# Attention output through weights of products in two output halves, and one setup step for the last mixers

## The reference

```python
s = jnp.einsum("bthd,bshd->bhts", qb, k) * scale      # fox, a block of 128 queries
s = s + fb[..., :, None] - big_f[..., None, :]
s = jnp.where(k_pos[None, :] <= q_pos[:, None], s, -jnp.inf)
p = jax.nn.softmax(s, axis=-1)
return jnp.einsum("bhts,bshd->bthd", p, v)
...
sa = jnp.einsum("bhvk,bhk->bhv", state, -kk_t)        # rwkv, the mixer that runs beside it
state = (state * w_t[:, :, None, :] + sa[..., None] * (kk_t * a_t)[:, :, None, :]
         + v_t[..., None] * k_t[:, :, None, :])
```

```python
c = _rms_norm(a_ckv, kv_norm_g[layer])
lb_all = jnp.cumsum(jax.nn.softmax(lb_logits, axis=0), axis=0)
o_a = _dsa_mixer(a_q, c, a_iq, a_ik, a_iw, w_uk[layer], rel_bias)   # index scores, top 256, softmax
o_b = _hgrn2_mixer(b_q, b_f, b_i, lb_all[layer])
```

## Time and profile before

| | |
|---|---|
| time, median of 3 runs | 5380.27 us (5369.63 to 5392.05) |
| profiled execution | 5369.74 us, span 5368.1 us |
| mean granted clock of TensorE | 0.829 of 2.4 GHz |
| TensorE products busy | 4420.3 us (82% of the span) |
| VectorE, ScalarE, GpSimd busy | 2632.6, 1913.5, 738.0 us |
| fox and rwkv steps | from 1372.9 us to 2514.4 us of the span |
| setup of the second layer's mixers | from 3517.4 us to 3575.7 us of the span |

### The profile page before, as it was taken

How to read it: one execution, slowest core, us unless ns; L and a number is a source line. 1 busy time by engine, 2 the same in 40 slices (tenths; PEclk the granted TensorE clock), 3 DMA queues, 4 the chain that set the end, 5 groups by cost and what they waited for, 6 DMA issues and landing times. The chain is left out here.

```text
span 5368.1 us, 64565 instructions
## 1 busy us (share of the span) xinstructions
PE 4420.3 (82%) x23178; PEld 3238.0 (60%) x23178; DVE 2632.6 (49%) x5352; ACT 1913.5 (36%) x3894; POOL 738.0 (14%) x753
## 2 busy tenths in 40 slices
PE   7988999973678888987998999956688887876668
PEld 6876777762566666665446888833344454544557
DVE  3114444445555544542111111148998888887435
ACT  3112233234223223332111010123676767777511
POOL 3101111100000000000000000012222333444310
PEclk9998999975667677776999999976587887877779
DMA  5336666643010000001221212120000001011032
GB/s 180 124 123 231 210 209 216 215 155 123 24 34 23 23 23 12 23 14 69 85 84 69 81 65 81 54 61 23 17 19 18 18 18 36 18 36 36 30 129 103
DMA packets 199360, 417.95 MB, mean 78 GB/s; under 512 B 37032, under 2 KB 67404, under 8 KB 198876
## 3 DMA queue, kind: packets, MB, share of 16 engines
q1 hardware_dynamic: 199040, 413.81, 22.5%
HBM read 292.08 MB, written 121.65 MB: 77 GB/s over the span
## 5 line engine op out<-in xcount | busy, mean ns | idle before, releaser
L3131 POOL TENSOR_TENSOR ds_E<-ds_bT 128x256 f32<-128x256 f32 x112 | 71.8, 641 | 2928.5 <-ACT ds_bT L3100 2743.2
L2620 PE MATMUL ds_big<-ds_ikT,ds_iqT 64*128 64x512 f32 (+3 forms) x640 | 384.0, 747 | 94.9 <-ACT ds_iqT L2597 60.2
L272 PE MATMUL g_acc<-g_ws_hi,second_hT_hi 128*128 128x512 f32 (+1 forms) x1024 | 384.5, 375 | 11.8 <-DVE g_ws_lo L307 11.8
L273 PE MATMUL g_acc<-g_ws_lo,second_hT_hi 128*128 128x512 f32 (+1 forms) x1024 | 384.2, 375 | 0.0
L274 PE MATMUL g_acc<-g_ws_hi,second_hT_lo 128*128 128x512 f32 (+1 forms) x1024 | 384.1, 375 | 0.0
L475 PE MATMUL mm_big<-mm_gw_hi,mm_ghT_hi 128*128 128x512 f32 (+1 forms) x768 | 318.5, 415 | 31.2 <-PEq L134 31.2
L2683 DVE TENSOR_SCALAR_CACHE_REDUCE ds_eq<-ds_hi,ds_num 128x2048 uint16<-128x2048 uint16 (+13 forms) x224 | 331.3, 1479 | 26.2 <-issue 4.0
L286 DVE COPY g_stage<-g_acc 128x512 f32<-128x512 f32 (+1 forms) x64 | 41.6, 650 | 529.0 <-PE g_acc L274 529.0
L477 PE MATMUL mm_big<-mm_gw_hi,mm_ghT_lo 128*128 128x512 f32 (+1 forms) x768 | 299.7, 390 | 0.0
L476 PE MATMUL mm_big<-mm_gw_lo,mm_ghT_hi 128*128 128x512 f32 (+1 forms) x768 | 299.3, 390 | 0.0
L2723 ACT ACTIVATE ds_signs<-ds_lo,ds_at 128x2048 bf16<-128x2048 uint16 (+13 forms) x224 | 291.4, 1301 | 1.5 <-issue 0.4
(11 more groups left out here) (505 smaller groups left out, 10007.3 us busy)
## 6 DMA issues: line engine op xcount, KB each, us to landing
mm_ghT_hi<-turned SPq DMA_DIRECT2D x96, 512.0 KB, 4.0
mm_ghT_lo<-turned SPq DMA_DIRECT2D x96, 512.0 KB, 5.3
proj<-g_stage SPq DMA_DIRECT2D x112, 256.0 KB, 2.0
proj<-mm_gstage SPq DMA_DIRECT2D x80, 256.0 KB, 5.0
mm_x<-proj SPq DMA_DIRECT2D x64, 256.0 KB, 3.8
g_w<-in_w_in SPq DMA_DIRECT2D x56, 256.0 KB, 4.0
proj<-fp_stage SPq DMA_DIRECT2D x48, 256.0 KB, 2.0
mm_graw<-in_w_in SPq DMA_DIRECT2D x40, 256.0 KB, 6.5
```

Source lines behind the costliest of these rows:

```text
L272: pe.matmul(sums, hT.hi[:, k, tile], wt.hi[:, k, 0:width], start=(k == 0), stop=False)
L273: pe.matmul(sums, hT.hi[:, k, tile], wt.lo[:, k, 0:width], start=False, stop=False)
L2620: pe.matmul(big[:, n % 2, 0:wd], iqT[o, h // 2], b.ikT[o, x:x + wd], start=True, stop=True)\
```

## The change

Two edits are joined.

**Values as weights.** In steps with five key tiles or more (k from 4 to 15) the roles in `weigh` are exchanged. The values of a tile (128 keys by 64 dimensions) become the stationary operand, and the transposed softmax weights (128 columns) move. The result of an even tile goes to partitions 0 to 63 of bank 7 and that of an odd tile to partitions 64 to 127, so the two sums of a head lie in two output halves (`sums`), with dimensions on the partitions. At the end of the step ScalarE copies the bank to SBUF (`f_sums_kept`), and four products with `fold` (two identity matrices on top of each other) add the halves and turn them back to token order in bank 5 or 6. VectorE waits for these (`f_folded`) before it divides. `fold` is made by one VectorE instruction ahead of the steps.

**One setup step.** `last_mixers_setup` does in one step what `load`, the norm step, `hgrn_setup`, `threshold_setup` and the step of loads did. All 15 loads are issued at its start, and each engine waits for those that it needs. The temporary buffers of the old norm step are now places in buffers that the tiles use later. Half of the index-key transposes move ahead of the bias products and the other half behind them, and the copy of the transposed index keys moves from VectorE to ScalarE, in two parts.

```diff
@@ fox_attend
-    o = big[:, 7, 0:GW].rearrange("p (h d) -> p h d", h=HEADS)
+    sums = big[:, 7].rearrange("p (h t) -> p h t", h=HEADS)
+
+    folded = k >= FOLDED
...
+    if folded:
+        uses.append((("o",), None))
     turns = in_turn([5, 6], uses)
+    o = big[:, turns["o",][0] if folded else 7, 0:GW].rearrange("p (h d) -> p h d", h=HEADS)
...
         yield from keep(act, HEADS - 1)
+        if folded:
+            yield 11 / N
+            act.wait_ge(s.f_weighed, HEADS * NP)
+            act.activation(pT[:, 0], sums, ACT.Copy).then_inc(s.f_sums_kept, 1)
...
         yield 11 / N
         dve.wait_ge(s.f_exps, HEADS)
         dve.reciprocal(den[:], den[:])
-        dve.wait_ge(s.f_weighed, HEADS * NP)
+        if folded:
+            dve.wait_ge(s.f_folded, 1)
+        else:
+            dve.wait_ge(s.f_weighed, HEADS * NP)
...
+        if folded:
+            yield 11 / N
+            take(pe, "o")
+            pe.wait_ge(s.f_sums_kept, 1)
+            for h in range(HEADS):
+                m = pe.matmul(o[:, h], pT[:, 0, h], b.fold[:], start=True, stop=True)
+            m.then_inc(s.f_folded, 1)
...
         for t in range(wd // P):
-            m = pe.matmul(o[:, h], pT[:, (h * NP + p) % 2, t], b.v[:, x // P + t, h * HD:(h + 1) * HD],
-                          start=(p == 0 and t == 0), stop=(x + (t + 1) * P == W))
+            at = x // P + t
+            v, w = b.v[:, at, h * HD:(h + 1) * HD], pT[:, (h * NP + p) % 2, t]
+            if folded:
+                m = pe.matmul(sums[(LOW, HIGH)[at % 2], h], v, w, start=(at < 2), stop=(at + 2 > k))
+            else:
+                m = pe.matmul(o[:, h], w, v, start=(at == 0), stop=(at == k))
         m.then_inc(s.f_weighed, 1)
```

The new setup step, cut to its loads and the order of its work:

```diff
+        @block.sync
+        def _(sp):
+            for r in range(2):
+                sp.dma_start(ik[:, :, r], proj[:, E_IK:E_IK + IDX_DIM].rearrange("(t p) c -> p t c", p=P))\
+                  .then_inc(s.ik_in, 16)
+            sp.dma_start(ct[:], proj[:, E_C:E_C + R].rearrange("(t p) c -> p t c", p=P)).then_inc(s.c_in, 16)
+            sp.dma_start(g, row(w['kv_norm_g_2'])).then_inc(s.g_in, 16)
+            sp.dma_start(rb, w['rel_bias_2'], allow_slow_non_contiguous=True).then_inc(s.oh_in, 16)
+            sp.dma_start(oh, onehot).then_inc(s.oh_in, 16)
...
+            n = index_loads(ib, sp, s.rest_in, proj, TILES - 1) + attend_loads(ab, sp, s.rest_in, proj, TILES - 1)
+            n += hgrn_loads(hb, sp, s.rest_in, proj, 0)
+            sp.dma_start(ab.uk[:], w['w_uk_2'].rearrange("h d r -> d h r")).then_inc(s.rest_in, 16)
+            sp.dma_start(ab.uv[:], w['w_uv_2'].rearrange("h r v -> r h v")).then_inc(s.rest_in, 16)
+            sp.wait_ge(s.bias_kept, 1)
+            sp.dma_start(table, ot).then_inc(s.table_out, 16)
+            sp.wait_ge(s.rest_in, n + 32)
+            sp.wait_ge(s.table_out, 16)
...
+            dve.wait_ge(s.biases, 1)
+            dve.tensor_copy(ot.rearrange("h (a b) -> h a b", a=5), big[0:HEADS, 0:5]).then_inc(s.bias_kept, 1)
+            dve.wait_ge(s.lb_in, 48)
+            dve.tensor_tensor(top, lb[:, 0], lb[:, 1], ALU.max)
+            dve.drain()
+            for n in range(2):
+                dve.tensor_tensor(lb[:, n], lb[:, n], top, ALU.subtract)
+            dve.drain().then_inc(s.diffd, 1)
+            dve.wait_ge(s.turned, 1)
+            dve.tensor_copy(cT[:].rearrange("p (a b) -> p a b", a=4), big[:, 0:4]).then_inc(s.kept, 1)
...
+            for n in range(2):
+                act.wait_ge(s.ik_t, n + 1)
+                act.activation(ikT[:].rearrange("p (a b) -> p a b", a=4)[:, 2 * n:2 * n + 2],
+                               big[:, (5, 0)[n]:(7, 2)[n]], ACT.Copy).then_inc(s.ik_kept, 1)
...
+        @block.tensor
+        def _(pe):
+            pe.wait_ge(s.ik_in, 32)
+            for t in range(8):
+                m = pe.transpose(big[:, 5 + t // 4, (t % 4) * P:(t % 4 + 1) * P],
+                                 ik[:, t].rearrange("p r d -> p (r d)"), c.ident)
+            m.then_inc(s.ik_t, 1)
+            pe.wait_ge(s.oh_in, 32)
+            for k in range(5):
+                m = pe.matmul(big[0:HEADS, k], rb, oh[:, k * 512:(k + 1) * 512], start=True, stop=True)
+            m.then_inc(s.biases, 1)
+            pe.wait_ge(s.bias_kept, 1)
+            for t in range(8, TILES):
+                m = pe.transpose(big[:, t // 4 - 2, (t % 4) * P:(t % 4 + 1) * P],
+                                 ik[:, t].rearrange("p r d -> p (r d)"), c.ident)
+            m.then_inc(s.ik_t, 1)
+            pe.wait_ge(s.ik_kept, 2)
+            pe.wait_ge(s.normed, 1)
+            for t in range(TILES):
+                m = pe.transpose(big[:, t // 4, (t % 4) * P:(t % 4 + 1) * P], ct[:, t], c.ident)
+            m.then_inc(s.turned, 1)
...
-        hgrn_setup(nc, w, hb)
-        threshold_setup(nc, tb)
-        with step(nc, "arrived") as (block, s):
...
+        last_mixers_setup(nc, c, w, proj, table, onehot, ib, tb, ab, hb)
```

More of the change, by code:

```diff
@@ L1024, in fox_rwkv_and_gating @@
         fb.qT, fb.kT, fb.v, fb.z = qT, kT, v, B.sb("z", [P, 2, GW])
+        fb.fold = B.sb("fold", [P, HD])
         rb = rwkv_early_buffers(B)
@@ L1029, in fox_rwkv_and_gating @@
             ub = sgu_buffers(nc, c, E, w)
-            with step(nc, "sgu_in gains_in ahead_in turned masked scaled cleared") as (block, s):
+            with step(nc, "sgu_in gains_in ahead_in turned masked scaled cleared folds") as (block, s):
                 @block.sync
@@ L1051, in _ @@
                     dve.memset(carry[:], 0.0).then_inc(s.cleared, 1)
+                    dve.tensor_tensor(fb.fold[:], c.ident[:, LOW], c.ident[:, HIGH], ALU.add).then_inc(s.folds, 1)
                     dve.wait_ge(s.gains_in, 48)
@@ L1142, in fox_buffers @@
     b.y = B.sb("y", [P, 2, HEADS, HD])
+FOLDED = 4
 def fox_attend(c, b, s, proj, k):
@@ L2639, in threshold_buffers @@
     return b
-def threshold_setup(nc, b):
-    with step(nc, "start_set") as (block, s):
-        @block.vector
-        def _(dve):
-            dve.memset(b.at[:, 2:3], -32767.5).then_inc(s.start_set, 1)
 SELECT_SIGNALS = "low_found "
```

134 lines of the change are left out of this document (45 added, 89 removed).

## The result

The changed kernel takes 5354.31 us (median of 6 runs, 5347.53 to 5360.55) against 5381.91 us (6 runs) for the kernel before: a ratio of 0.9945, 95% interval 0.9927 to 0.9963. A second series, with its own runs of before, gave 5345.65 against 5380.96 us, 0.9941 (0.9920 to 0.9962). So it is faster by 28 to 35 us. The forecast was -61 us.

A forecast was written before the change was run, and what follows sets the result against it. Above a floor of about 57 us a step from rwkv's chain, TensorE's list was taken as the bound. Value passes -46, tail +27, clock -25 and setup -17 gave -61 us from 5380.27: 5319 us, range 5262 to 5390 us.

The forecast's parts named there:

- The passes in pairs: Value passes of steps 4 to 15: output halves run side by side, 648 slots for 1008 passes, saving 52 us of TensorE.
- The step's -46 us: Value passes of steps 4 to 15: the 52 us of TensorE saved, times 0.88, shorten the kernel by 46 us.
- the factor 0.88: Fox steps: each us of TensorE work changes the step by 0.88 us, read from steps 3 and 15.
- rwkv's chain sets a floor: Fox steps: rwkv's chain keeps each step at about 57 us or more; above that TensorE's list is the bound.
- Weight loads: Value passes: loads overlap products in flight although they use the same rows, so they do not stop the pairing.
- the rival built on that rule: Value passes: bare weight loads and halves in turns, 1.4 us a group, +66 us, 5446 us; chance 0.06.
- The tail, +27 us: Ends of the twelve steps: folding products and later division add 1.9 to 2.7 us each, +27 us (23 to 33).
- The setup, -17 us: Setup ahead of the second layer's tiles: the joined step brings the first tile's work 17 us earlier (12 to 20).
- The clock, -25 us: Steps 4 to 15: fewer, denser slots make TensorE's clock rise earlier, -25 us (nothing to 65).
- the clock gives nothing: Rival for the fox steps: halves in pairs but the clock rises where it did, -36 us, 5344 us; chance 0.16.
- the bound of 65: Far end of the clock's gain: 8 us in each of the eight longest steps, 65 us, giving 5279 us; chance 0.13.

The follow-up runs named there:

- setup_only: The kernel before with the new setup step alone, old value products kept: 5373.47 us, ratio 0.9989 to before.
- no_fold: The changed kernel without the copy of the sums and the four folding products, so fox's result is wrong: 5327.90 us, ratio 0.9907 to before.
- one_half: The changed kernel with all tiles' results in the lower output half, copy and folding products on 64 rows: 5335.52 us, ratio 0.9921 to before.
- fox_only: The changed kernel with the old setup, so values as weights alone: 5373.29 us, ratio 0.9987 to before.
- setup_again: setup_only measured once more, the kernel before with the new setup step alone: 5369.26 us, ratio 0.9979 to before.
- wide: setup_only with each old value product moving two heads' values, 128 columns instead of 64, half unused, division in two operations: 5319.52 us, ratio 0.9872 to before.
- before_again: The kernel before, unchanged, executed once more for a second trace: 5402.64 us in that single execution.
- fox_again: fox_only, unchanged, executed once more for a second trace: 5370.19 us in that single execution.

## Why the prediction was wrong, step by step

**The passes in pairs** (8 passes of four tiles in about 0.55 us): right, 0.58 us. The saving of 52 us of TensorE was 44 us in the profiles of before and after, and 50.9 us at nearly equal clock (149.7 in setup_only, 98.8 in no_fold). The window of steps 4 to 15 of no_fold, and its group of value passes:

```profile
1604.60:2479.60 875.00, 753.55 (x6240) 527.04 (x6240) 443.35 (x1104) 285.97 (x540) 0.00 (x0) 0.73 0.06 20
```

```profile
L1279 PE MATMUL fox_big<-fox_pT,fox_v 128*64 128x128 f32 x1008 | 98.8, 320 | 1.0
```

The step's -46 us is best read from these two kernels as well, which differ in the value passes alone: -41 to -46 us in the medians, and -30.9 us in steps 4 to 15 (between -25 and -42 with the other traces of the old form). So the saved TensorE time was right, and the factor 0.88 is not confirmed: by the two traces 0.6 of it came out in the steps. The rest of the medians' gain lies outside them: between the same two traces the tiles, which are the same, are 13.5 us shorter (1536.8 against 1550.3), with a cause left open (below). One sentence of the reading behind the 0.88 was wrong, that VectorE stays under half of the step: in step 3 it is busy for 32.40 of 57.20 us. That rwkv's chain sets a floor there was not tested.

**Weight loads**: right. Each load has all 128 rows, as had the products in flight, and still the pairs kept their pace. The Trainium skill (TensorE: Matmul & The Clock Gate, "The mechanism") says in its list that a load overlaps products in flight only if its row group differs. This case's trace disagrees: the rival built on that rule had 1.4 us for a group, and 0.58 was measured. Of the halves the Trainium skill's page TensorEngine Tiling (Array Packing), "Key Properties", says that tiles work independently; one_half (1.02 us) beside the changed kernel (0.58) agrees.

**The tail, +27 us**: the place was right and the size near. A step ends 1.9 to 2.1 us later in most cases (near the lower of the bounds 1.9 and 2.7), and all twelve together 24.5 us later than before and 25.3 us later than in no_fold. In the lengths of steps 4 to 15 the fold costs 32.0 us by one trace each (changed kernel less no_fold; 21.9 with fox_only's trace), in the medians 17.8. Of the medians' 17.8, one number in the order of VectorE's list takes away some 16.

**The setup, -17 us**: right in its stage, -18.5 us. Its chain was as forecast, except that the keys were issued 1.8 us behind the start in place of 4.0, and took 8.6 us to land in place of 7.5; the biases stayed the later. Of the whole kernel's time setup_only and setup_again give only 6 and 12 us, since their tiles run longer, at a lower clock. Why the tiles do is not shown.

**The clock, -25 us**: this is the step that failed. "The new passes put the same results into fewer and denser slots, so the rise at 2454.30 should come earlier and the falls be fewer", taken at -25 us. In steps 4 to 15 the clock gave nothing: 508 us at 1.2 GHz after, 486 to 550 us in the traces of before, 507 in setup_only. Step 15, forecast near 80 us, took 90.2 at a clock of 0.71. The rival "the clock gives nothing", 5344 us, is the case that came true, 10 and 2 us below the two medians, but not for its reason. It said that the first half of the step stays as it is. What the runs show is that two effects cancel. A pass that moves 128 columns in place of 64 lifts the clock (one_half and wide: 135 and 147 us less at 1.2 GHz than setup_only). In wide this made the steps 48.7 us shorter, most of the bound of 65 that I had left aside. Pairing the same passes takes it back: 508 us against 372. Why pairing does so is not shown; what the runs show is the two times, and 473 against 360 us between no_fold and wide. The tail may add to it: no_fold has 35 us less at 1.2 GHz than the changed kernel, from one trace, where the changed kernel's own lie 24 us apart (484 to 508). Denser in results was not what counted. The row for it was there: in the earlier trace rows TensorE is busy for 49.29 of 51.20 us and is granted 0.50. The Trainium skill (TensorE: Matmul & The Clock Gate, "What's actually happening") says that the clock follows how busy TensorE has been. The busy share of the profile is no measure of that here: in step 15 of one_half it is 77.90 of 86.50 us at a clock of 0.82, in the changed kernel 80.15 of 90.20 at 0.71.

**The sum.** By medians: setup -6 (setup_only) or -12 (setup_again), passes and what they do to the clock -46 or -41 (no_fold less the same two), tail +18: -34 or -35, where -28 to -35 were measured. Each of these differences starts where the one before it ends, so that they add up is no test of them. The forecast without its clock term is -36, and that this comes so near is in part luck: the setup was put 5 to 11 us too high as a gain and the tail 9 us too high as a cost, and the two offset each other. The range of 5262 to 5390 us held both medians.

**Open.** Where the whole kernel's gain lies cannot be read from one pair of profiles. The fox steps 4 to 15 of the changed kernel are 907.0 us in its trace, against 899.7 in the trace of before and 916.6 in before_again. The tiles are 1531.5 against 1541.5 and 1544.5. What lies ahead of step 4 is touched by no more than one small instruction in any kernel here with 64 columns in steps 0 to 3, and it took 1597.2 us (fox_again) to 1612.5 us (before_again). The tiles meet the clock in another state with each edit, and that may be what moves them by up to 23 us; no run here tells it apart.

## What to carry to other kernels

Before you make a stream of products shorter, look at the clock that it is granted: where it stands at 1.2 GHz although TensorE is busy, a pass bound by its weight load can move more columns at nearly no cost and bring the clock up, even if the results are thrown away (here 48.7 us in twelve steps, about 1% of the kernel's time). A layout that halves the slots can give that back. Price such an edit by medians of several executions: here single traces of one program differ by 10 to 17 us in the same twelve steps. And when you add a wait to an instruction, look at what stands behind it in its engine's list: in the changed kernel one place further back was worth about as much as leaving out the whole fold. In one_half the same move ended each step as much sooner and brought nothing, so try it in the kernel where it is to stay.

## What the runs showed of the hardware that was not expected

- A pass of float32 that loads 128 columns has nearly one pace with 64 and with 128 moving columns: 16 in 1.89 us with 64 at 2.4 GHz, eight in 0.99 us with 128. Over steps 4 to 15 its group even gets shorter with more columns, 149.7, 145.0 and 140.4 us for 64, 96 and 128.
- The clock of the same stretch was 0.72, 0.76 and 0.79 with 64, 96 and 128 columns.
- Two products in two output halves run side by side although both use all 128 rows, and the order of the halves within four tiles changes nothing (0.58 and 0.60 us for eight passes; 1.02 us in one half).
- The tiles of the second layer, unchanged in every kernel here, took 1527.1 to 1550.5 us. Step 14 of the kernel before took 91.1 us in one execution and 106.3 in another.
